# Two 16-head attentions of a two-block kernel: the probabilities times the values as one float32 matmul, the exponentials kept in SBUF, the scores computed two pairs ahead

## The reference

```python
# layer 0: 8 heads A (2 key/value heads shared by 4 query heads each) and 8 latent heads B (keys 96 wide)
sc = jnp.einsum('bkgqd,bksd->bkgqs', qblk, kt).astype(jnp.float32) * scale
p = jax.nn.softmax(sc, axis=-1).astype(vt.dtype)
o = jnp.einsum('bkgqs,bksd->bkgqd', p, vt)
# layer 1: 16 heads, each query sees a window of 8 x 16 tokens, with a bias per offset
sc = jnp.einsum('bhqd,bhqkd->bhqk', qblk, kg).astype(jnp.float32) * scale + bias[None]
p = jax.nn.softmax(sc, axis=-1)
o = jnp.einsum('bhqk,bhqkd->bhqd', p, vg)
```

## Time and profile before

| what | us |
|---|---|
| median of 3 runs | 1153.97 (1153.74 to 1155.96) |
| the profiled execution, its own time | 1155.43 |
| its span, first to last instruction | 1153.6 |
| TensorE busy, share of the span | 1134.4 (98%) |
| VectorE busy | 846.3 (73%) |
| ScalarE busy | 628.2 (54%) |
| GpSimd busy | 496.8 (43%) |
| granted TensorE clock, mean | 0.997 of full speed |

### The profile page before, as it was taken

How to read it: one execution, slowest core, us unless ns; L and a number is a source line. 1 busy time by engine, 2 the same in 40 slices (tenths; PEclk the granted TensorE clock), 3 DMA queues, 4 the chain that set the end, 5 groups by cost and what they waited for, 6 DMA issues and landing times.

```text
span 1153.6 us, 18456 instructions
## 1 busy us (share of the span) xinstructions
PE 1134.4 (98%) x6922; PEld 1013.0 (88%) x6922; DVE 846.3 (73%) x1102; ACT 628.2 (54%) x858; POOL 496.8 (43%) x433
## 2 busy tenths in 40 slices
PE   8999999999999999999999999999999999999997
PEld 7999999888998888888897988888888888888886
DVE  4778988987875898777898777566666676656655
ACT  7544443656634665555668755444464677444443
POOL 2699998897101643333233628880010455000000
PEclk9999999999999999999999999999999999999999
DMA  9555555563457456555542287656555513665550
GB/s 301 192 179 180 185 177 183 182 218 110 130 165 237 155 183 211 189 174 182 159 150 96 76 233 244 186 189 208 182 176 190 181 38 125 204 198 193 193 182 37
DMA packets 142809, 201.06 MB, mean 174 GB/s; under 512 B 3301, under 2 KB 123109, under 8 KB 142749
## 3 DMA queue, kind: packets, MB, share of 16 engines
q1 hardware_dynamic: 141776, 196.88, 51.6%
q0 software_dynamic: 912, 3.17, 1.2%
q10 hardware_dynamic: 60, 0.20, 0.1%
HBM read 199.20 MB, written 1.05 MB: 174 GB/s over the span
## 4 chain that ended last, share of the span: by engine, by line
PE 90%; DVE 3%; issue 2%; POOL 2%; ACT 2%; DMA 0%; POOLq 0%; ACTq 0%; DVEq 0%
PE ps L2024 51%; PE ps L2061 21%; PE ps L2066 11%; PE ps L2170 3%; PE ps L2232 1%; POOL wlo L485 1%; PE ps L2220 1%; PE ps L2152 1%; POOL merged L600 0%; DMA x<-in_x 0%; DVE work L1305 0%; PE ps L2138 0%; ACT ps L761 0%; DVE p_parts L1237 0%; DVE kreg L1556 0%
## 5 line engine op out<-in xcount | busy, mean ns | idle before, releaser
L1210 DVE TENSOR_TENSOR wlo<-raw,whi 128x2048 fp32r<-128x2048 f32 (+1 forms) x162 | 376.9, 2327 | 131.0 <-ACT whi L671 130.1
L671 ACT ACTIVATE whi<-raw 128x2048 fp32r<-128x2048 f32 (+1 forms) x178 | 337.4, 1897 | 140.7 <-PE ps L2024 133.8
L2061 PE MATMUL ps<-p_parts,whi 128*128 128x512 f32 x1184 | 289.3, 390 | 0.0
L2061 PEld LDWEIGHTS ps<-p_parts,whi 128*128 128x128 f32 x1184 | 220.0, 188 | 44.8
L2024 PE MATMUL ps<-p_parts,whi 128*128 128x256 f32 x912 | 164.8, 283 | 0.6 <-DVE p_parts L1237 0.6
L2066 PE MATMUL ps<-p_parts,wlo 128*128 128x256 f32 x1184 | 163.3, 282 | 0.0
L2066 PEld LDWEIGHTS ps<-p_parts,wlo 128*128 128x128 f32 x1184 | 155.8, 191 | 5.5
L2024 PE MATMUL ps<-whi,q_hi 128*128 128x512 f32 x380 | 148.6, 391 | 0.2 <-POOL wlo L485 0.2
L2024 PE MATMUL ps<-whi,q_lo 128*128 128x512 f32 x380 | 148.3, 390 | 0.0
L2024 PE MATMUL ps<-wlo,q_hi 128*128 128x512 f32 x380 | 147.9, 389 | 0.0
L2024 PEld LDWEIGHTS ps<-p_parts,whi 128*128 128x128 f32 x912 | 142.3, 192 | 1.1 <-issue 1.0
(11 more groups left out here) (321 smaller groups left out, 1833.5 us busy)
## 6 DMA issues: line engine op xcount, KB each, us to landing
raw<-in_w_in SPq DMA_DIRECT2D x35, 1024.0 KB, 5.0
raw<-in_w_up SPq DMA_DIRECT2D x22, 1024.0 KB, 5.1
raw<-in_up_a SPq DMA_DIRECT2D x16, 1024.0 KB, 5.4
raw<-in_down_a SPq DMA_DIRECT2D x16, 1024.0 KB, 4.9
raw<-in_up_b SPq DMA_DIRECT2D x16, 1024.0 KB, 5.4
raw<-in_down_b SPq DMA_DIRECT2D x16, 1024.0 KB, 4.9
raw<-in_od_w_qkv SPq DMA_DIRECT2D x12, 1024.0 KB, 5.1
raw<-in_w_down SPq DMA_DIRECT2D x11, 1024.0 KB, 5.0
```

The lines of the kernel that those rows point to most:

```text
L671: nc.scalar.activation(whi[:, g % R, 0:n], raw[:, g % R, 0:n], ACT.Copy).then_inc(hi_ready, 1)
L1210: nc.vector.tensor_tensor(wlo[:, g % R, 0:n], raw[:, g % R, 0:n], whi[:, g % R, 0:n].bitcast(F32), ALU.subtract).then_inc(lo_ready[g % R], 1)
L2061: return nc.tensor.matmul(bank(2 * pb + h), whi[:, r, at], p_parts[:, :, S * k:S * k + S], start=k == 0, stop=False)
```

## The change

The first attention, of 4 heads ("att1"), keeps its form. For att2 and att3:

- The values product (7) is four plain float32 matmuls per pair in place of twelve in float32r: stationary operand 128x64 (one head's values, unsplit, straight from the projection's tile), moving 128x256 (the transposed rows, unsplit), and each head writes its own 64 partitions of bank 3. The splits of the values, the zeros beside them and the splits of the transposed rows go.
- The transposed rows are copied from bank 2 to SBUF once, of even heads by VectorE, of odd heads by ScalarE (`rows_out`), into four places.
- The exponentials are written to SBUF (`exp_rows`, four places; in att3 they lie where the biased scores lie). The scores of a head wait only for the exponentials (att2) or the maxima (att3) of the head two before it. The scores run two pairs ahead instead of one.
- The division reads SBUF alone: two one-source products of 128x256 with a reciprocal per row, in place of one of 128x512 with a broadcast operand. Its access pattern visits the even, then the odd elements.
- In att3 GpSimd also makes the upper parts of the queries and keys from pair 3 on; `lo(G_EVO)`, a lower part of a 1 MB group, moves from VectorE to GpSimd.

```diff
+        turned_rows = [misc[:, 1024 + 512 * n:1536 + 512 * n] for n in range(4)]
+        exp_rows = [a.rearrange("p (t n) -> p t n", t=T) for a in (work[:, 0:512], work[:, 2048:2560],
+                                                                   misc[:, 3072:3584], misc[:, 3584:4096])]
...
             def woven_heads(name):     # gpsimd
...
                 def queries_keys(u):
+                    if name == "att3" and u >= 3:
+                        pool.wait_ge(at_s, n0 + H * (u - 1))
+                        for src, up, low in unit_parts(u, units[u], H)[0]:
+                            last = nc.gpsimd.tensor_copy(up, src)
+                        last.then_inc(qk_hi, 1)
                     pool.wait_ge(qk_hi, u0 + u + 1)
                     lower(unit_parts(u, units[u], H)[0]).then_inc(qk_lo, 1)
...
                 if name == "att2":
+                    lo(G_EVO)
                     queries_keys(2)
...
             def exponentials(name, i):     # scalar
...
+                if name != "att1" and i >= 4:
+                    act.wait_ge(at_p, n0 + i - 3)
                 for t in range(T):
                     scored = bank(S_BANK[name] + i % 2, t * S, t * S + S)
-                    src = bsc[:, i % 2, t, :] if biased else scored
-                    last = nc.scalar.activation(scored, src, ACT.Exp,
+                    dst = scored if name == "att1" else exp_rows[i % 4][:, t, :]
+                    last = nc.scalar.activation(dst, dst if biased else scored, ACT.Exp,
...
+                def rows_out(i):
+                    act.wait_ge(at_t, n0 + i + 1)
+                    if i >= 4:
+                        act.wait_ge(at_v, n0 + i - 3)
+                    b = rows_bank(name, i)[0]
+                    nc.scalar.activation(turned_rows[i % 4], bank(b), ACT.Copy).then_inc(bank_read[b], 1)
...
                 for u in range(PAIRS):     # scalar
                     if u == 0 and name == "att2":
+                        rows_out(0)
                         exponentials(name, 2)
                     if u:
                         output_upper(u - 1)
+                    rows_out(2 * u + 1)
+                    if u == 0 and name == "att2":
+                        exponentials(name, 3)
+                        hi_half(G_EVO + 1, 0)
...
+                    if u + 3 < PAIRS and name == "att2":
...
                         queries_keys(name, u + 3)
+                    if u + 2 < PAIRS:
+                        exponentials(name, 2 * u + 4)
+                        exponentials(name, 2 * u + 5)
...
             def divided(name, i):     # vector
...
+                for t in range(T):
+                    last = nc.vector.tensor_scalar(by_twos(prob[:, i % 3, t, :]), by_twos(exp_rows[i % 4][:, t, :]),
+                                                   inv[:, t, :], None, ALU.mult)
+                last.then_inc(at_p, 1)
...
                 for u in range(PAIRS):     # vector
+                    if u == 0 and name == "att3":
+                        maxima(name, 2)
+                        maxima(name, 3)
+                        lo(G_V + 5)
                     if u:
+                        rows_out(2 * u)
                     if u + 1 < PAIRS:
                         divided(name, 2 * u + 2)
                     if u == 0 and name == "att2":
                         latent_keys_in((5,))
+                    if u:
+                        output_lower(u - 1)
                     if u + 1 < PAIRS:
                         divided(name, 2 * u + 3)
                     if u == 0 and name == "att2":
                         latent_keys_in((6, 7))
+                    if u + 2 < PAIRS:
+                        maxima(name, 2 * u + 4)
+                        maxima(name, 2 * u + 5)
...
             def pair_scores(name, u):     # tensor
...
-                    pe.wait_ge(at_p, n0 + 2 * u)
+                    pe.wait_ge(at_nm if biased else at_e, n0 + 2 * u)
...
+                def pair_times_values(u):
+                    if u in (0, PAIRS // 2):
+                        for b, uses in values_in(name, u):
+                            free(b, uses)
+                    for i in (2 * u, 2 * u + 1):
+                        b, uses = rows_bank(name, i)
+                        free(b, uses + 1)
                     free(3, USES[name][3] + u)
                     for m in range(2):
+                        for h in range(2):
+                            rows = turned_rows[(2 * u + h) % 4]
+                            ins = nc.tensor.matmul(ps[HD * h:HD * h + HD, 3, 0:S], units[u]["v"][:, m, h, :], rows[:, S * m:S * m + S],
+                                                   start=m == 0, stop=m == 1)
+                            if m == 1:
+                                ins.then_inc(at_v, 1)
...
                 for u in range(PAIRS + 1):
+                    if 0 < u < PAIRS:
                         rows_transposed(name, 2 * u, *rows_bank(name, 2 * u))
+                    if u:
+                        pair_times_values(u - 1)
                     if u < PAIRS:
                         rows_transposed(name, 2 * u + 1, *rows_bank(name, 2 * u + 1))
+                    if u + 2 < PAIRS:
+                        pair_scores(name, u + 2)
+                    if u > 1:
+                        half_of_output(u - 2, 1)
                     if u:
                         half_of_output(u - 1, 0)
                 half_of_output(PAIRS - 1, 1)
```

More of the change, by code:

```diff
@@ L317, in two_blocks, with values_in @@
         WEIGHTS_LO_DVE = {"att2": {11: G_EVO + 3, 15: G_F2A}, "att3": {}}
[L319 to L325, removed]
+        def values_in(name, u):
+            if name == "att2":
+                return [(b, USES["ev_in"][b] + 1) for b in (5, 7)] if u == 0 else [(b, USES["ukv"][b] + 1) for b in range(4, 8)]
+            return [(b, USES["v"][b] + 1) for b in ((4, 6) if u == 0 else (5, 7))]
         def unit_sides(u, H):
@@ L614, in _ @@
             inverse_root("n_mix2a")
-            for b in (5, 7):
-                pool.wait_ge(bank_read[b], USES["ev_in"][b] + 1)
-            values_of("att2", 0)
             pool.wait_ge(h_ms, 1)
@@ L623, in _ @@
                                         in1=mhalf[:, 0:2], op=ALU.pow).then_inc(l_r, 1)
-                if part == 0:
-                    pool.wait_ge(slot_used, G_LAT + 3)
-                    values_of("att2", 1)
             woven_heads("att2")
@@ L737, in values @@
                 split_upper([unit_parts(u, units[u], H)[1]]).then_inc(v_hi, 1)
-            def zeros_beside_values(parts):
-                for part in parts:
-                    gap = part[:, UNIT_V:UNIT_V + T * 256].rearrange("p (t n) -> p t n", t=T)[:, :, HD:P]
-                    nc.scalar.activation(gap, ident[:, :].rearrange("p (t n) -> p t n", t=T), ACT.Copy,
-                                         scale=0.0).then_inc(v_zero, 1)
             def hi_half(g, n):
@@ L1364, in woven_heads, with rows_out @@
                     lo(G_V + 4)
+                def rows_out(i):
+                    dve.wait_ge(at_t, n0 + i + 1)
+                    if i >= 4:
+                        dve.wait_ge(at_v, n0 + i - 3)
+                    b = rows_bank(name, i)[0]
+                    nc.vector.tensor_copy(turned_rows[i % 4], bank(b)).then_inc(bank_read[b], 1)
                 for u in range(PAIRS):
-                    rows_lower(name, 2 * u)
+                    if u == 0 and name == "att3":
+                        maxima(name, 2)
+                        maxima(name, 3)
+                        lo(G_V + 5)
                     if u:
-                        output_lower(u - 1)
-                    if u + 1 < PAIRS and not (u == 0 and name == "att2"):
-                        maxima(name, 2 * u + 2)
-                        maxima(name, 2 * u + 3)
-                    if u == 0 and name == "att3":
-                        lo(G_V + 5)
-                    if u == 1:
-                        rows_lower(name, 2 * u + 1)
+                        rows_out(2 * u)
                     if u + 1 < PAIRS:
```

109 lines of the change are left out of this document (18 added, 91 removed).

## The result

The changed kernel takes 1161.16 us (median of 4 runs, 1160.21 to 1161.99), the kernel before 1154.03 beside it: a ratio of 1.0056, 95% interval 1.0045 to 1.0068. It is slower by 0.6%, where 1152.1 and "no change" were forecast, and 0.2 us above the range of 8 in 10, which ended at 1161.0. The profiled execution took 1161.54 us, with a span of 1159.6.

A forecast was written before the change was run, and what follows sets the result against it. TensorE, busy 98% of the span, was taken as the bound. Values product -0.2, standing time -1.7 and the rest nothing gave -1.9 us on the median of 1153.97, so 1152.1; range of 8 in 10 from 1147.0 to 1161.0.

The forecast's parts named there:

- What bounds the kernel: Whole kernel: TensorE is busy for 98% of the span, so only its work or standing time can move the total much.
- Part 1: Values product of 16 pairs: a pair costs 1.41 us against 1.42 before, in all -0.2 us, a wash.
- its own sign of being wrong: Values product: the forecast is wrong if a block differs from 1.41 us by more than 0.15.
- the fifth slot: Values product: eight passes of two heads form a staircase of five slots of 0.21 us, 1.06 in all.
- The price of changing tiles: Values product: changing to half-size tiles and back costs 0.35 us per pair, taken from the scores' row halves.
- The first rival: Values product: column halves pair up fully, tile change some 0.2, 1.05 us a pair; total 1146.4 us; chance 0.18.
- The second rival: Values product: column halves do not overlap; 1162.4 us with the tile change, 1156.8 without; chances 0.16 and 0.10.
- Part 2: TensorE's standing time in att2 and att3: 4.9 us before, 3.1 and 0.1 after, so 1.7 us less.
- some 1.7: Third attention: att3 gets shorter by some 1.7 us, att2 by nothing.
- from -4 to +0.5: Total time: spread in us around the forecast, which has chance 0.42; half of it lies beyond the 0.2%.
- Part 3: Work of VectorE, GpSimd and ScalarE, including the output weights' lower part on GpSimd (4.61 us): costs nothing.
- Cost: nothing: VectorE's division as two products: at most 0.8 us a round, hidden beside TensorE; 11 us were that cover gone.

The follow-up runs named there:

- the kernel with all places reordered: The changed kernel with w_evo's lower part back on VectorE and six queue places changed in the second and third attentions: 1157.53 us, ratio 1.0029.

## Why the prediction was wrong

**What bounds the kernel** was right: TensorE, and only its work and its waits counted.

**Part 1** was right that the halves overlap and wrong in how far: a pair costs 1.23, not 1.41, so 16 pairs gain about 3 us and not 0.2 (4 us by the 0.25 of a whole round). That is off by more than the 0.15 that the prediction set as its own sign of being wrong. The step that failed is the fifth slot, from "In order, pass 2 of head 0 must follow its pass 1, and head 1's first pass can start only beside it": the records show four slots, some 0.215 each as forecast, 0.86 in all, and exchanging the loops changed nothing. The price of changing tiles, carried over from the row halves as 0.35, was right: 1.23 - 0.86 = 0.37. The first rival had the overlap right and the change of tiles too low (0.2, in all 1.05 a pair). The second rival, that the halves don't overlap, gave 1162.4 and 1156.8: near the measured time, for a cause that the records exclude.

**Part 2** was right in its two places and incomplete. The wait for the exponentials of head 3, forecast 1.6, is 1.69; the one for the copy of head 2, forecast 1.2, is 1.17. Missing was the 2.21 us wait for GpSimd: the scores of pair 4 come a round earlier, and their lower parts stand behind weight pieces in GpSimd's queue. In the third attention 0.1 was forecast, and 0.56 and 1.46 are there, the second since `values_out(1)` stands behind more of ScalarE's work. The last round of att2 has one of 0.83 for VectorE's copy, behind half of a weight. The middle rounds have no wait, as forecast, in this profile; in that of the exchanged loops they have. Att3 got shorter by 1.80, where "some 1.7" was forecast from waits that go: the match is luck, since the waits grew (2.0 shown against 1.7) and the rounds of 5.9 in place of 6.2 made the gain. Two slips changed no verdict: 0.78 is VectorE's share in the second attention, whose round is 6.51 and not 6.2, and the spread "from -4 to +0.5" is counted from the kernel before, not from the forecast.

**Part 3 is the step that failed**: "GpSimd stands idle for 12.33 us just there, its splits for pair 2 come right behind and are needed only at 620.8: nothing". The idle time of GpSimd was read as free time. Here it was not: a VectorE instruction with two SBUF inputs fell into it, on TensorE's path, and took 4.01 us for 0.15. Undoing this part gave back 4.45 us, and adding it to the kernel before cost 5.6. "Cost: nothing" for the division was the same error: VectorE's mean share has room, but its products stand for GpSimd's whole instructions, which put the kernel with all places reordered at no gain. The trace before did show the exclusion in small, at this very operation. It runs twice, and the first time, at 603.32, it took 0.35 us and ended with a GpSimd cast (603.26 + 0.39 = 603.65; 603.32 + 0.35 = 603.67):

```profile
603.32 0.35 DVE L1854 TENSOR_TENSOR stat<-stat 128x2 f32<-128x2 f32 x1 [0.59 <-POOL stat L622]
```

```profile
603.26 0.39 POOL L513 CAST p_parts<-gates 128x256 fp32r<-128x256 f32 x1
```

And the other way round, a GpSimd cast of 128x256 at 654.72 took 0.76 us beside a two-input subtraction of VectorE, and 0.39 to 0.41 in twelve of the thirteen other places. The prediction did not take this in.

Of the 9.25 us in att2 the rows give: 3.8 more of standing behind the 128x2 operation (4.00 against 0.22 before, at 614.75); about 2.3 in the latent transposes at the low clock (from 617.04 to 623.32 are 6.28 us, before 3.95 from 614.75 to 618.70); 1.6 in nine 512-wide matmuls (from 638.82 to 642.46 are 3.64 us, at 0.23 each they are 2.07); and some 3.5 of other waits, which are shown as 1.69, 1.17, 0.20, 2.21 and 0.83. Counted from start to start, as the prediction counted those before, they are 6.5, against 3.0 before without the 0.22. The shorter rounds, values product included, take some 2.2 off (8 x 0.28). That is 9.0 of the 9.25. How much of each the low clock takes differs from run to run.

## What to carry over

Idle time of GpSimd beside a busy VectorE was not free here: before moving work there, list VectorE's instructions with two SBUF inputs or one-source SBUF-to-SBUF products in that stretch, and ask whether one of them is on the path. Cutting the moved instruction up shared the wait out over as many victims, and delaying such instructions moved the collision; it gave back 3.1 us in one order of the queues and nothing in another. A gain in the steady rounds (0.28 us in a middle round of either attention) is easily spent at the starts, where one queue place costs 1 to 2 us and a wait of 4 brings down the clock as well; moving single places there moved the waits, and only fewer GpSimd instructions, with some of the new places, made the change pay.

## What was not expected of the hardware

- A VectorE operation on 128x2 elements took 4.01 us beside a GpSimd instruction of 4.61, and a product of 128x256 was kept waiting through five GpSimd instructions (6.59 us for the two products of a head, 0.62 alone).
- Float32 matmuls with 64 stationary columns, on the two column halves of the array, overlapped fully in both orders of the queue that were run: eight passes in four slots of some 0.22 us.
- Behind a wait of 2.3 us among several others TensorE's granted clock was 0.77 in one execution and 1.00 in another of the same code; the slower one took 3.2 us longer in the second attention.
